# Second half of the first modulation by quarters, a third weight between them, and weight parts one step ahead of the convolutions

## The chip, the cores and the metric

The kernel runs on one core of a Trainium2 chip. Its measure is the device time of one execution in microseconds (us), median of three runs. The core has TensorE (PE, the matrix products), ScalarE (ACT), VectorE (DVE), GpSimd (POOL) and SyncE (SP, which here only issues DMAs); each runs its own list of instructions in order, and they meet at semaphores.

## What is computed

Two transformer blocks follow one another, on one sequence of 256 tokens with 1024 features, in float32. The change lies in the first steps of the first block:

```python
mod = (c_act @ w_ada[l] + b_ada[l])[:, None, :]
shift1, scale1, gate1, shift2, scale2, gate2 = jnp.split(mod, 6, axis=-1)
h = rms_norm(x, norm1_w[l]) * (1.0 + scale1) + shift1
proj = h @ w_in[l]
gq, gk, gv, gz, ga, gb, sq, sk, sv = jnp.split(proj, split_points, axis=-1)
qkv = jax.nn.silu(causal_depthwise_conv(jnp.concatenate([gq, gk, gv], axis=-1), conv_w[l]))
```

`c_act` is one vector of 1024 values, so `scale1` and `shift1` are two vector-matrix products over 8 MB of `w_ada`. Nothing of `h` can be had before they are known for its features, and no product with `w_in` can begin before some of `h` is there. What follows (a gated delta rule, window attention, an MLP, then a second block pair) isn't changed.

## The kernel before

**Weights.** They come as blocks of 1024 KB (`load` on SP, into the three buffers of `raw`). A float32 product is made of three products of rounded parts (`three`, L1715: high by high, high by low, low by high). So each weight block w is split first: ACT writes the high part (`hi(w)`, L669, one instruction of 128x2048), then DVE the low part (`lo(w)`, L1072). Each of the three buffers for parts is used again three blocks later, so `hi(w)` waits until PE is done with block w-3 (`FORMER`, semaphore `block_used`). `h` is split likewise (`h_high`, `first_low`), tile by tile: tile k holds 128 of the 1024 features.

**The start.** PE fills its first microseconds with products of zeros (`warm`). The first modulation is made in two halves of the features. For half 0 and half 1 SP loads four pieces of 1024 KB each (`load_ada`: scale rows 0-511 and 512-1023, then shift rows 0-511 and 512-1023), into the buffers `AT`, `qkT`, `X_inv` and `keys_queries`. For the first three, PE (`ada`, L1827) makes products with four column groups of the array side by side, 512 features wide; ACT copies the rows (`mod_rows_copy`), and PE sums over the partitions and turns them to a column (`row_sums`, 16 one-column matmuls). The fourth piece goes straight to columns (`last_columns`, 64 one-column matmuls). DVE makes scale and shift of it (`first_scales`, `first_shifts`), then `h` (`first_scaled`, `first_low`).

With half 0 known, PE does k = 0 to 3 of the first two weight blocks (`column_half`). k = 4 to 7 of both wait for half 1. The loop `for w in range(6)` follows (L1924): `project(w)` completes block w, a block being 48 matmuls of 256 columns. After block 0 come the gate product (`gab_wh`, `gab_wl`, 24 matmuls) and a small product for a table (`rel_bias`), after block 1 two transposes, after block 4 the sums of the decay (`tri` by `g`, waits `gate_done`). In the middle of block 6, `first_sums` (L2011) waits for `decay_dve`.

**The loop beside it on ACT and DVE.** ACT at step w (L750): `hi(w + 2)`, then the copy of block w out of PSUM into `pad` (waits `block_used`), then `feature(w - 1)`: Silu and, for four of them, Square of the convolution before. DVE at step w (L1218): `lo(w + 2)`, then the convolution of block w, eight instructions (L1233 and L1240; waits `pad_ready` for its block and `feature_ready` for the one before, since both share `cacc`). Step 1 and step 2 hold the gate computation besides, step 5 the difference that gives `decay_dve`. ACT loads function tables where it goes from one function to another (L745, L767, L771).

**SP's order.** `x`, half 0 of the modulation, weights 0 and 1, half 1, then, once the third piece of half 1 has landed, weight 2 and the rest.

Of the kernel before, what the change touches and what calls it, by code (L numbers as in the profile page):

```python
# [9 lines left out]
P = 128  # L10
# [19 lines left out]
FIRST_WEIGHTS = 2  # L30
# [289 lines left out]
def build(nc, stream, x_in, consts_in, vectors_in, gab_in, t5_onehot, t5_log, rel_bias, out):  # L320
    t5_scratch = nc.dram_tensor("t5_scratch", (16, 384), F32, kind="Internal")
    with ExitStack() as ctx:
# [81 lines left out]
        mod_rows = [[inv_b[:, 1024 * i + 512 * u:1024 * i + 512 * u + 512] for u in range(2)] for i in range(2)]  # L404
# [142 lines left out]
        def _(sp):  # L547
# [9 lines left out]
            def load_ada(half, i):  # L557
                if half and i < 3:
                    sp.wait_ge(s.ada_used, i + 1)
                elif half:  # L560
                    sp.wait_ge(s.rows_summed, 2)
                k, c = 4 * (i % 2), 512 * half + (D if i < 2 else 0)
# [10 lines left out]
            for i in range(4):  # L573
                load_ada(0, i)
# [79 lines left out]
        def _(act):  # L654
# [58 lines left out]
            def mod_rows_copy(half, u):  # L713

                act.wait_ge(s.ada_used, 3 * half + (3 if u else 2))
                act.activation(mod_rows[half][u], B[u][:, :], ACT.Copy).then_inc(s.rows_copied, 1)

            def first_highs(w, quarters):
                r = weight_load(w)
                act.wait_ge(raw_landed[r % RING], (r // RING + 1) * 16)  # L720
                for q in quarters:
                    act.activation(high_of(w)[:, 2 * q:2 * q + 2, :], raw_of(r)[:, 2 * q:2 * q + 2, :], ACT.Copy).then_inc(s.first_hi, 1)
# [13 lines left out]
            mod_rows_copy(1, 0)  # L736
            mod_rows_copy(1, 1)
            h_high(0, range(4, KD))
# [11 lines left out]
            for w in range(6):  # L750
                hi(w + 2)
# [31 lines left out]
            hi(8)  # L783
# [280 lines left out]
        def _(dve):  # L1064
# [64 lines left out]
            def first_scales(half):  # L1129
                c, at = slice(4 * half, 4 * half + 4), 480 + 8 * half  # L1130
                dve.wait_ge(s.rows_summed, 2 * half + 1)
                link(dve.tensor_tensor(a1[:, c], STAT[:, at:at + 4], b_scale[:, c], ALU.add))
                dve.tensor_tensor(a1[:, c], a1[:, c], vecs("norm1")[:, c], ALU.mult).then_inc(s.mod_ready, 1)

            def first_shifts(half):
                c, at = slice(4 * half, 4 * half + 4), 484 + 8 * half
                dve.wait_ge(s.rows_summed, 2 * half + 2)
                dve.tensor_tensor(mods[:, c], STAT[:, at:at + 4], vecs("b_ada")[:, c], ALU.add).then_inc(s.mod_ready, 1)
                dve.wait_ge(s.mod_ready, 2 * half + 2)

            def h_parts_2():
                dve.wait_ge(s.rstd_ready, 2)
                dve.wait_ge(s.mod_ready, 6)
# [17 lines left out]
            def residual(last):  # L1161

                for m in range(KD):
# [4 lines left out]
                    if m == 0:  # L1168
                        dve.wait_ge(s.mod_ready, 5)
# [39 lines left out]
            first_scales(1)  # L1209
            first_shifts(1)  # L1210
            for k in range(4, KD):
                first_scaled(k)
                if k > 4:
                    first_low(k - 1)
            first_low(KD - 1)


            for w in range(6):  # L1218
# [5 lines left out]
                lo(w + 2)  # L1224
# [62 lines left out]
            lo(8)  # L1287
# [416 lines left out]
        def _(pe):  # L1704
# [16 lines left out]
            def column_half(w, bank, ks):  # L1721

                if ks[0] == 4:
                    pe.wait_ge(s.lo_ready, w + 1)
                wh = high_of(w)
                wl = low_of(w)
                for k in ks:
                    if k in (0, 2):
                        pe.wait_ge(s.first_lo, 3 * w + k // 2 + 1)
                    pe.wait_ge(s.h_lo_ready, k + 1)  # L1730
# [96 lines left out]
            def ada(half, i):  # L1827

                pe.wait_ge(ada_landed[i], 16 * (half + 1))
                if half and i % 2 == 0:  # L1830
# [726 lines left out]
```

## Time and profile before

| | us |
|---|---|
| median of 3 runs | 991.53 (991.39 to 992.0) |
| the profiled execution | 990.9 |
| its span in the profile | 989.1 |
| PE busy | 978.5 (99%) |
| DVE busy | 607.8 (61%) |
| ACT busy | 476.8 (48%) |

The profile has the time of each instruction on each engine. Times in its rows count from the start of the span. A row of the timeline is one run of like instructions: start, length, engine, line, operation, output and inputs, how many; a bracket at its end gives the idle time of the engine just before, and what ended it. A busy PE need not be a useful one: `zero_r` products count as busy. Line numbers are those of the kernel before.

### The profile page before, as it was taken

What the parts mean: (1) busy time and instruction counts of PE and PEld (TensorE: products, weight loads), DVE (VectorE), ACT (ScalarE), POOL (GpSimd) and SP (SyncE); (2) the same over time, 40 slices, a digit from 0 to 9 for tenths busy, and PEclk for the clock granted to TensorE, in tenths of its full rate; (3) what the DMA queues carried; (4) which work ended last, traced back from release to release, by engine and by line L of the source; (5) the groups of instructions that cost most, each with busy time, mean ns of one, the idle gap of its engine ahead of it and who ended that gap; (6) DMA issues with size and microseconds to landing.
All of it is one profiled execution on the core that took longest, in us unless ns stands there. A gap on an engine that the chain in (4) does not pass through costs nothing.

```text
span 989.1 us, 15628 instructions
## 1 busy us (share of the span) xinstructions
PE 978.5 (99%) x6703; PEld 847.0 (86%) x6703; DVE 607.8 (61%) x750; ACT 476.8 (48%) x640; POOL 36.8 (4%) x37
## 2 busy tenths in 40 slices
PE   9999999999999999999999999999999999999998
PEld 6799988978888888999888888889999888888886
DVE  2589988775665454787754545365876663545444
ACT  3485277454343435533354344446655563435343
POOL 0000560010000000000000000000000000000000
PEclk9999999999999999999999999999999999999999
DMA  9757324775767354446544645454643435454621
GB/s 345 284 191 259 122 87 151 270 243 214 278 217 285 132 211 172 171 171 214 211 145 153 216 167 206 177 191 153 226 156 130 139 144 185 180 204 166 216 86 43
DMA packets 31588, 185.70 MB, mean 188 GB/s; under 512 B 3040, under 2 KB 5536, under 8 KB 10784
## 3 DMA queue, kind: packets, MB, share of 16 engines
q1 hardware_dynamic: 29984, 180.37, 51.0%
q0 software_dynamic: 832, 3.17, 1.0%
q8 instruction: 53, 0.87, 0.3%
q10 hardware_dynamic: 704, 1.17, 0.3%
q14 instruction: 15, 0.12, 0.0%
HBM read 183.62 MB, written 1.07 MB: 187 GB/s over the span
## 4 chain that ended last, share of the span: by engine, by line
PE 98%; DVE 1%; ACT 0%; issue 0%; POOL 0%; DVEq 0%; POOLq 0%
PE bank L1706 51%; PE acc L1706 43%; PE bank L2308 1%; PE bank L2086 1%; PE bank L1802 0%; PE acc L1802 0%; PE acc L2086 0%; PE bank L2166 0%; PE bank L1979 0%; DVE inv_b L1391 0%; DVE norm_tmp L1511 0%; DVE silu_and_hid L1510 0%; DVE inv_b L1384 0%; PE acc L2316 0%; DVE X_inv L1435 0%
## 5 line engine op out<-in xcount | busy, mean ns | idle before, releaser
L1075 DVE TENSOR_TENSOR w_lo<-raw,w_hi 128x2048 fp32r<-128x2048 f32 x144 | 326.9, 2289 | 146.2 <-ACT w_hi L675 146.1
L1706 PE MATMUL bank<-w_hi,h_parts 128*128 128x512 f32 x1056 | 333.5, 391 | 1.3 <-DVE h_parts L1152 1.3
L675 ACT ACTIVATE w_hi<-raw 128x2048 fp32r<-128x2048 f32 x144 | 271.5, 1909 | 102.3 <-PE acc L1706 70.9
L1706 PEld LDWEIGHTS bank<-w_hi,h_parts 128*128 128x128 f32 x1056 | 198.2, 188 | 44.6 <-issue 2.0
L1706 PE MATMUL bank<-w_lo,h_parts 128*128 128x512 f32 x528 | 205.5, 389 | 0.0
L1706 PE MATMUL acc<-h_parts,w_hi 128*128 128x256 f32 x928 | 170.8, 286 | 0.6 <-DVE h_parts L1127 0.6
L1706 PEld LDWEIGHTS acc<-h_parts,w_hi 128*128 128x128 f32 x928 | 143.5, 190 | 5.3 <-issue 3.3
L1706 PE MATMUL acc<-h_parts,w_lo 128*128 128x256 f32 x464 | 131.2, 283 | 0.0
L1706 PE MATMUL acc<-w_hi,o_hi 128*128 128x512 f32 x296 | 119.1, 402 | 0.0
L1706 PEld LDWEIGHTS bank<-w_lo,h_parts 128*128 128x128 f32 x528 | 99.2, 188 | 19.8
L1706 PE MATMUL acc<-w_hi,o_lo 128*128 128x512 f32 x296 | 115.6, 391 | 0.0
L1706 PE MATMUL acc<-w_lo,o_hi 128*128 128x512 f32 x296 | 115.6, 390 | 0.0
L1706 PEld LDWEIGHTS acc<-h_parts,w_lo 128*128 128x128 f32 x464 | 88.0, 190 | 0.0
L927 ACT ACTIVATE silu_and_hid<-bank,rms 128x256 f32<-128x256 f32 x44 | 20.9, 475 | 105.2 <-PE bank L1706 105.2
L1550 DVE TENSOR_TENSOR o_lo<-bank,o_hi 128x512 fp32r<-128x512 f32 x33 | 22.8, 691 | 76.0 <-ACT o_hi L932 76.0
L1706 PEld LDWEIGHTS acc<-w_hi,o_lo 128*128 128x128 f32 x296 | 55.6, 188 | 12.4
L1706 PEld LDWEIGHTS acc<-w_hi,o_hi 128*128 128x128 f32 x296 | 55.6, 188 | 10.9 <-issue 0.2
L1706 PEld LDWEIGHTS acc<-w_lo,o_hi 128*128 128x128 f32 x296 | 55.7, 188 | 10.5
L932 ACT ACTIVATE o_hi<-bank 128x512 fp32r<-128x512 f32 x33 | 19.8, 599 | 75.2 <-PE bank L2308 75.2
L1542 DVE SCALAR_TENSOR_TENSOR silu_and_hid<-bank,rms,silu_and_hid 128x256 f32<-128x256 f32 x44 | 21.2, 481 | 36.6 <-ACT silu_and_hid L927 36.6
L1706 PE MATMUL bank<-h_parts,w_hi 128*128 128x256 f32 x192 | 34.7, 283 | 0.3 <-DVE h_parts L1520 0.3
L1706 PEld LDWEIGHTS bank<-h_parts,w_hi 128*128 128x128 f32 x192 | 29.4, 188 | 0.7 <-DVE h_parts L1520 0.5
(370 smaller groups left out, 993.3 us busy)
## 6 DMA issues: line engine op xcount, KB each, us to landing
raw<-stream SPq DMA_DIRECT2D x162, 1024.0 KB, 5.1
AT<-stream SPq DMA_DIRECT2D x2, 1024.0 KB, 11.8
qkT<-stream SPq DMA_DIRECT2D x2, 1024.0 KB, 13.0
X_inv<-stream SPq DMA_DIRECT2D x2, 1024.0 KB, 14.2
keys_queries<-stream SPq DMA_DIRECT2D x4, 512.0 KB, 12.4
t_tables<-t_scratch POOLq DMA_DIRECT2D x1, 2048.0 KB, 10.2
x_res<-x_in SPq DMA_DIRECT2D x2, 512.0 KB, 5.2
t_tables<-t_scratch POOLq DMA_DIRECT2D x1, 1024.0 KB, 12.4
```

Of the source, the lines that this page charges most:

```text
L675: act.activation(high_of(w), raw_of(r), ACT.Copy).then_inc(s.hi_ready, 1)
L927: act.activation(sg[:, T * t:T * t + T], B[t][:, 0:256], ACT.Silu, scale=rms[:, t:t + 1] if f else 1.0).then_inc(s.silu_ready, 1)
L932: act.activation(hid_parts(j)[0].rearrange("p a b -> p (a b)"), B[2][:, :], ACT.Copy).then_inc(s.hid_hi_ready, 1)
L1075: dve.tensor_tensor(low_of(w), raw_of(weight_load(w)), high_of(w), ALU.subtract).then_inc(s.lo_ready, 1)
L1542: dve.scalar_tensor_tensor(out=o, in0=up, scalar=rms[:, t:t + 1], in1=gate, op0=ALU.mult, op1=ALU.mult).then_inc(s.hid_ready, 1)
L1550: dve.tensor_tensor(low.rearrange("p a b -> p (a b)"), B[2][:, :], high.rearrange("p a b -> p (a b)"), ALU.subtract).then_inc(s.hid_lo_rea ...
L1706: return pe.matmul(o, l, r, start=start, stop=stop, skip_group_check=True)
L2086: ins = pe.transpose(bank[hh][:, P * i:P * i + P], sc[:, hh, P * i:P * i + P], perm)
L2308: ins = pe.transpose(B[2][:, T * i + P * t:T * i + P * t + P], hid[:, T * t + P * i:T * t + P * i + P], ident)
```

## The change

The first half of the modulation and all ahead of it stay. The second half (features 512 to 1023) is cut into two quarters, tiles 4-5 and 6-7. SP loads four pieces of 1024 KB again, now quarter 2 scale, quarter 2 shift, **weight 2**, quarter 3 scale, quarter 3 shift; each piece holds all 1024 rows of 256 features, so a run in memory is 1 KB instead of 2 KB. The fourth piece is done as the others, by `ada_quarter`; `last_columns` is left for half 0 alone. The wait of SP ahead of weight 2 is gone.

PE does k = 0 to 3 of block 2 too, k = 4, 5 of three blocks once quarter 2 is known, and the gate product in three portions (`gab_part`, now in bank `B[3]`); `warm(3)` and `warm(4)` are gone. `project(0)` to `project(2)` then have only k = 6, 7 left. ACT and DVE split blocks 2 and 3 in quarters (`FIRST_WEIGHTS = 4`), block 2 between the steps of the modulation. Block 3's high parts stand at ACT's step 0 of the loop; `hi(w + 3)` and `lo(w + 3)` take the place of `hi(w + 2)` and `lo(w + 2)`, and `hi(8)`, `lo(8)` behind the loop are gone.

```diff
-FIRST_WEIGHTS = 2
+FIRST_WEIGHTS = 4
+EARLY_LOADS = 3
+FEATURES = ((0, 4), (4, 6), (6, 8))
...
-            for i in range(4):
-                load_ada(1, i)
-            sp.wait_ge(ada_landed[2], 32)
-            for i in range(2, len(LOADS)):
+            load_quarter(2, 0)
+            load_quarter(2, 1)
+            load(2)
+            load_quarter(3, 0)
+            load_quarter(3, 1)
+            for i in range(EARLY_LOADS, len(LOADS)):
                 load(i)
...
             for w in range(6):
-                hi(w + 2)
+                if w + 3 < FIRST_WEIGHTS:
+                    first_highs(w + 3, (0, 1, 2, 3))
+                else:
+                    hi(w + 3)
...
-                    act.activation(gabT, B[0][0:16, 0:T], ACT.Copy).then_inc(s.gab_copied, 1)
+                    act.activation(gabT, B[3][0:16, 0:T], ACT.Copy).then_inc(s.gab_copied, 1)
...
-            hi(8)
...
-                lo(w + 2)
+                if w + 3 < FIRST_WEIGHTS:
+                    first_lows(w + 3, (0, 1, 2, 3))
+                else:
+                    lo(w + 3)
...
-            lo(8)
...
+            def ada_quarter(q, u):
+
+                i = 2 * (q - 2) + u
+                pe.wait_ge(ada_landed[i], 32)
+                pe.wait_ge(s.rows_copied, i + 1)
+                for k in range(KD):
+                    at = 32 * (k % 4)
+                    ins = mm(B[u][at:at + 32, 0:256], c_columns[:, k, :], ada_raw[i][:, 256 * k:256 * k + 256], k < 4, k >= 4)
+                ins.then_inc(s.ada_used, 1)
...
-            column_half(0, A[0], range(4))
-            ada(1, 0)
-            column_half(1, A[1], range(2))
-            ada(1, 1)
-            column_half(1, A[1], range(2, 4))
+            column_part(0, range(0, 4))
+            ada_quarter(2, 0)
+            column_part(1, range(0, 2))
             row_sums(1, 0)
-            ada(1, 2)
-            warm(3)
+            column_part(1, range(2, 4))
+            ada_quarter(2, 1)
+            gab_part(range(0, 4))
             row_sums(1, 1)
-            last_columns(1)
-            warm(4)
+            column_part(2, range(0, 4))
+            ada_quarter(3, 0)
+            column_part(0, range(4, 6))
+            row_sums(2, 0)
+            ada_quarter(3, 1)
+            column_part(1, range(4, 6))
+            row_sums(2, 1)
+            column_part(2, range(4, 6))
+            gab_part(range(4, 6))
```

PE before, from the third piece of half 1 to the first products of block 0 with half 1 (`X_inv` and `keys_queries` are the pieces, `inv_b` the copied rows, `zero_r` the zeros, `h_parts` the parts of `h`; names in brackets are semaphores):

```order
L1706 MATMUL bank<-X_inv,c_columns 32x512 [waits rows_copied,ada_landed2]
L1706 MATMUL bank<-X_inv,c_columns 32x512 x3
L1706 MATMUL acc<-zero_r 128x512 x3
L1706 MATMUL bank<-consts,inv_b 64x1 [waits mod_ready,rows_copied]
L1706 MATMUL bank<-consts,inv_b 64x1 x7
L1706 MATMUL bank<-c_act_sb,keys_queries 64x1 [waits ada_landed3]
L1706 MATMUL bank<-c_act_sb,keys_queries 64x1 x15
L1706 MATMUL bank<-c_act_sb,keys_queries 64x1 [waits ada_rest_landed]
L1706 MATMUL bank<-c_act_sb,keys_queries 64x1 x15
L1706 MATMUL acc<-zero_r 128x512 x4
L1706 MATMUL acc<-h_parts,w_hi 128x256 [waits h_lo_ready,lo_ready]
```

PE after the change, from the last piece (quarter 3, shift) on:

```order
L1736 MATMUL bank<-keys_queries,c_columns 32x256 [waits rows_copied,ada_landed3]
L1736 MATMUL bank<-keys_queries,c_columns 32x256 x7
L1736 MATMUL acc<-h_parts,w_hi 128x256 [waits h_lo_ready,first_lo]
L1736 MATMUL acc<-h_parts,w_hi 128x256
L1736 MATMUL acc<-h_parts,w_lo 128x256
L1736 MATMUL acc<-h_parts,w_hi 128x256 x2
L1736 MATMUL acc<-h_parts,w_lo 128x256
```

The 32 one-column matmuls of `last_columns` and the zeros are gone from this place; the piece is now eight matmuls of 256 columns, and products of a weight block stand right behind them.

ACT before, from the last tiles of `h` (`L702`) to the first Silu (`inv_p` is `pad`, `probsT` the gate product's copy):

```order
L702 ACTIVATE h_parts<-norm_tmp 128x256 [waits t_ready] x4
L675 ACTIVATE w_hi<-raw 128x2048 [waits raw_landed2]
L759 ACTIVATE inv_p<-acc 128x2x256 [waits pool_zeroed,block_used]
L764 ACTIVATE probsT<-bank 16x256 [waits gab_product]
L675 ACTIVATE w_hi<-raw 128x8x256 [waits block_used,raw_landed0]
L753 DMA consts<-consts_in 128x1664
L759 ACTIVATE inv_p<-acc 128x2x256 [waits conv_done,block_used]
L745 ACT_TABLE_LOAD
L745 ACTIVATE keys_queries<-XT 128x512 [waits conv_done]
```

ACT after the change, the same place:

```order
L713 ACTIVATE h_parts<-norm_tmp 128x256 [waits t_ready] x2
L736 ACTIVATE w_hi<-raw 128x2x256 [waits block_used,raw_landed0]
L736 ACTIVATE w_hi<-raw 128x2x256 x3
L781 ACTIVATE inv_p<-acc 128x2x256 [waits pool_zeroed,block_used]
L786 ACTIVATE probsT<-bank 16x256 [waits gab_product]
L686 ACTIVATE w_hi<-raw 128x8x256 [waits block_used,raw_landed1]
L775 DMA consts<-consts_in 128x1664
L781 ACTIVATE inv_p<-acc 128x2x256 [waits conv_done,block_used]
L764 ACT_TABLE_LOAD
L764 ACTIVATE keys_queries<-XT 128x512 [waits conv_done]
```

The high part written ahead of the first copy into `pad` was block 2's, with no wait on PE; now it is block 3's, in four instructions, and the first of them waits for `block_used`, that is, for the end of PE's block 0.

## Rows read from the trace of the kernel before

**Rows 1.** The page: busy us, share of the span and instructions of each engine.

```profile
PE 978.5 (99%) x6703; PEld 847.0 (86%) x6703; DVE 607.8 (61%) x750; ACT 476.8 (48%) x640; POOL 36.8 (4%) x37
```

**Rows 2.** PE's waits from 60 to 220 us: total us, times, longest.

```profile
PE bank L1706 <- DVE h_parts L1152: 1.3, 1, 1.3
PE bank L1706 <- DVE X_inv L1435: 1.2, 1, 1.2
```

**Rows 3.** Timeline of PE: start us, us, engine, line, operation, count.

```profile
31.83 1.06 PE L1706 MATMUL bank<-qkT,c_columns 128*32 128x512 f32 x8
...
34.45 0.63 PE L1706 MATMUL bank<-consts,inv_b 128*64 128x1 f32 x16
35.01 1.07 PE L1706 MATMUL bank<-X_inv,c_columns 128*32 128x512 f32 x8
36.00 0.96 PE L1706 MATMUL acc<-zero_r 128*128 128x512 f32 x3
...
37.38 2.01 PE L1706 MATMUL bank<-c_act_sb,keys_queries 128*64 128x1 f32 x64
39.32 1.20 PE L1706 MATMUL acc<-zero_r 128*128 128x512 f32 x4
41.11 0.47 PE L1706 MATMUL acc<-h_parts,w_hi 128*128 128x256 f32 x2 [0.59 <-DVE h_parts L1127]
...
47.69 0.51 PE L1706 MATMUL acc<-h_parts,w_hi 128*128 128x256 f32 x2
...
50.95 0.51 PE L1706 MATMUL acc<-h_parts,w_hi 128*128 128x256 f32 x2
...
68.14 0.73 PE L1706 MATMUL bank<-g,consts 128*128 128x8 f32 x6
...
77.45 1.10 PE L1706 MATMUL bank<-consts,X_inv 128*64 128x2 f32 x32
```

**Rows 4.** Timeline of SP: the issues of two pieces of half 1.

```profile
12.24 0.38 SPq L565 DMA_DIRECT2D AT<-stream  x1
14.81 0.38 SPq L565 DMA_DIRECT2D qkT<-stream  x1
```

**Rows 5.** The same two in the DMA view: KB each, us from issue to landing.

```profile
AT<-stream SPq DMA_DIRECT2D x1, 1024.0 KB, 15.0
qkT<-stream SPq DMA_DIRECT2D x1, 1024.0 KB, 15.1
```

**Rows 6.** Timeline of ACT: high quarters, copies into `pad`, the table, the Silu.

```profile
28.15 1.14 ACT L722 ACTIVATE w_hi<-raw 128x512 fp32r<-128x512 f32 x2
...
50.84 0.60 ACT L759 ACTIVATE inv_p<-acc 128x512 f32<-128x512 f32 x1 [1.61 <-PE acc L1706]
51.46 1.28 ACT L745 ACT_TABLE_LOAD   x1
52.75 0.63 ACT L745 ACTIVATE keys_queries<-XT 128x512 f32<-128x512 f32 x1
...
57.01 0.60 ACT L759 ACTIVATE inv_p<-acc 128x512 f32<-128x512 f32 x1 [1.15 <-DVE XT L1240]
```

**Rows 7.** Timeline of DVE: low quarters, shift, convolutions 0 to 2, gates, decay.

```profile
26.70 3.70 DVE L1190 TENSOR_TENSOR w_lo<-raw,w_hi 128x512 fp32r<-128x512 f32 x6
...
39.44 0.16 DVE L1138 TENSOR_TENSOR mods<-bank,vec 128x4 f32<-128x4 f32 x1 [3.96 <-PE bank L1706]
...
46.45 0.61 DVE L1233 TENSOR_SCALAR XT<-inv_p,vec 128x256 f32<-128x256 f32 x2
...
53.92 0.62 DVE L1233 TENSOR_SCALAR XT<-inv_p,vec 128x256 f32<-128x256 f32 x2 [2.28 <-ACT keys_queries L745]
...
59.54 0.61 DVE L1233 TENSOR_SCALAR XT<-inv_p,vec 128x256 f32<-128x256 f32 x2
...
63.67 0.17 DVE L1269 SCALAR_TENSOR_TENSOR g<-gate_tmp 128x16 f32<-128x16 f32 x1
...
75.87 0.17 DVE L1223 TENSOR_TENSOR kds<-bank,Gs 128x8 f32<-128x8 f32 x1
```

More of the change, by code:

```diff
@@ L555, in load, with load_quarter, load_half @@
                 sp.dma_start(raw[:, i % RING, :], stream[LOADS[i][2]]).then_inc(raw_landed[i % RING], 16)
-            def load_ada(half, i):
-                if half and i < 3:
+            def load_quarter(q, u):
+                i = 2 * (q - 2) + u
+                if i < 3:
                     sp.wait_ge(s.ada_used, i + 1)
-                elif half:
+                else:
                     sp.wait_ge(s.rows_summed, 2)
-                k, c = 4 * (i % 2), 512 * half + (D if i < 2 else 0)
+                c = 256 * q + (0 if u else D)
+                sp.dma_start(ada_raw[i].rearrange("p (k c) -> p k c", k=KD),
+                             stream[0:KD, :, c:c + 256].rearrange("k p c -> p k c")).then_inc(ada_landed[i], 16)
+            def load_half(i):
+                k, c = 4 * (i % 2), D if i < 2 else 0
                 rows = ada_raw[i].rearrange("p (k c) -> p k c", k=4)
@@ L711, in _, with mod_rows_copy @@
             root(0)
-            def mod_rows_copy(half, u):
-                act.wait_ge(s.ada_used, 3 * half + (3 if u else 2))
-                act.activation(mod_rows[half][u], B[u][:, :], ACT.Copy).then_inc(s.rows_copied, 1)
+            def mod_rows_copy(part, u):
+                a, b = FEATURES[part]
+                act.wait_ge(s.ada_used, 2 * part + u + 2)
+                act.activation(mod_rows[part][u], B[u][:, 0:P * (b - a)], ACT.Copy).then_inc(s.rows_copied, 1)
             def first_highs(w, quarters):
@@ L736, in _ @@
             mod_rows_copy(1, 0)
+            first_highs(2, (0, 1))
             mod_rows_copy(1, 1)
-            h_high(0, range(4, KD))
+            h_high(0, range(4, 6))
+            first_highs(2, (2, 3))
+            mod_rows_copy(2, 0)
+            mod_rows_copy(2, 1)
+            h_high(0, range(6, KD))
             dest = [kT[:, 0:2, :], kT[:, 2:4, :], qT[:, 0:2, :], qT[:, 2:4, :], vT[:, 0:2, :], vT[:, 2:4, :]]
@@ L1209, in _ @@
             first_scales(1)
+            first_lows(2, (0, 1))
             first_shifts(1)
[L1211 to L1215, printed above, removed]
+            first_scaled(4)
+            first_scaled(5)
+            first_low(4)
+            first_low(5)
+            first_lows(2, (2, 3))
+            first_scales(2)
+            first_shifts(2)
+            first_scaled(6)
+            first_scaled(7)
+            first_low(6)
+            first_low(7)
             for w in range(6):
@@ L1825, in _, with ada_half @@
             two = lambda b: b[:, :].rearrange("p (a b) -> p a b", a=2)
-            def ada(half, i):
-                pe.wait_ge(ada_landed[i], 16 * (half + 1))
-                if half and i % 2 == 0:
-                    pe.wait_ge(s.rows_copied, 1 + i // 2)
+            def ada_half(i):
+                pe.wait_ge(ada_landed[i], 16)
                 for k in range(4):
@@ L1857, in last_columns, with gab_part @@
                 ins.then_inc(s.rows_summed, 1)
+            def gab_part(ks):
+                pe.wait_ge(s.x_scaled, KD)
+                pe.wait_ge(s.gab_lo, 1)
+                for k in ks:
+                    pe.wait_ge(s.h_lo_ready, k + 1)
+                    a, b = gab_wh[:, 16 * k:16 * k + 16], gab_wl[:, 16 * k:16 * k + 16]
+                    ins = three(B[3][0:16, 0:T], a, b, h_hi[:, k, :], h_lo[:, k, :], k == 0, k == KD - 1)
+                if ks[-1] == KD - 1:
+                    ins.then_inc(s.gab_product, 1)
             def warm(n, bank=A[3]):
@@ L1918, in project @@
                 wait_bank(w)
-                if w < 2:
-                    column_half(w, A[w], range(4, KD))
+                if w < EARLY_LOADS:
+                    column_part(w, range(6, KD))
+                elif w < FIRST_WEIGHTS:
+                    column_part(w, range(KD))
                 else:
@@ L1926, in _ @@
                 if w == 0:
-                    pe.wait_ge(s.gab_lo, 1)
-                    for k in range(KD):
-                        a, b = gab_wh[:, 16 * k:16 * k + 16], gab_wl[:, 16 * k:16 * k + 16]
-                        ins = three(B[0][0:16, 0:T], a, b, h_hi[:, k, :], h_lo[:, k, :], k == 0, k == KD - 1)
-                    ins.then_inc(s.gab_product, 1)
+                    gab_part(range(6, KD))
                     pe.wait_ge(s.t5_loaded, 48)
```

74 lines of the change are left out of this document (40 added, 34 removed).

## The prediction

> **What bounds the kernel now.** The page gives PE 99% of the span [rows 1], but zeros count there, so I read on. PE's waits from 60 to 220 us come to two, 1.3 and 1.2 us [rows 2]; everything else that ACT and DVE do there is ready in time. The kernel is bound by how early PE gets through useful products, and by anything that ACT or DVE deliver late. So I ask two things of the change: how much of PE's time at the start it turns into useful products, and whether ACT and DVE keep up afterwards.
>
> In the timeline of PE [rows 3] the second half of the modulation is seen to cost, between 35.01 and 41.11 us: a piece (0.99), zeros (0.96), the row sums, 64 one-column matmuls for the last piece (2.01 busy, 1.94 to the next row), zeros (1.20) and an idle 0.59 until DVE has `h`. Zeros and the wait are what a filled schedule can win.
>
> **Prices on PE.** Blocks 2 to 4 are 144 matmuls of 256 columns from 50.95 to 68.14, 0.1194 us each [rows 3]. A piece of 512 columns takes 0.99 (35.01 to 36.00); with 12 matmuls behind it 2.62 (31.83 to 34.45), so 0.19 more go where products follow a piece. I take that gap behind row sums as well, bounds 0 and 0.19. Sixteen row-sum matmuls take 0.56 (34.45 to 35.01); a quarter has eight, 0.30. A piece by quarters is twice as many matmuls of half as many columns. The same columns stream, so 0.99 is the lower bound; if each cost as much as a wide one it would be 1.98. I take 1.0, since 64 one-column matmuls in 1.94 us show that issuing costs only 0.03 each.
>
> **PE in the new order.** Up to the point 31.83 both orders have done the same (12 products of block 1 behind the first piece). From there to the end of block 0 the new order has 102 products (12.18: 12 of block 1, 12 of the gates, 24 of block 2, 12 each of blocks 0, 1 and 2 with quarter 2, 6 gates, 12 of block 0 with quarter 3), three pieces (3.0), four row sums (1.2) and six gaps (1.14): 17.5, so block 0 ends at about **49.35**, against 44.0 before (41.11 plus 24 products). I call this moment t0. Behind it come 6 gate products (0.72), the table product (0.80: 6.58 from 41.11 to 47.69 less 48 products), 12 products with the transposes (1.82, half of the products of 47.69 to 50.95 and all of its rest), and 12 more: 4.85. Block 2 ends at 54.2, before at 56.7 (50.95 plus 48 products). **PE is 2.5 us ahead.**
>
> **What covers it.** The last shift and `h` behind it take 1.67 us (39.44 [rows 7] to 41.11 [rows 3]); the new order has 12 products of block 2, a gap and 6 of the gates there, 2.34, so no wait, 0.67 to spare. Quarter 2's shift has 24 products of block 2 and a piece over it. DMA: pieces of 2 KB runs land at 27.24 and 29.91 (12.24 + 15.0, 14.81 + 15.1) [rows 4, 5], 2.67 apart. For 1 KB runs the bounds are 2.67 (bytes decide) and 5.34 (runs decide); bytes are the nearer by far if 12 MB are to flow as they do, and I take 3.0. Weight 2 ahead of quarter 3 then puts the last piece near 39, and PE wants it at 42.6. Only above some 3.9 us for a piece would PE wait. SP loses a wait and gains one load that has none; behind it weight 3 lands near 42, long before t0. Cost zero.
>
> **ACT and DVE behind t0.** Here I find the price. Block 0 ends 5.3 us later than before, and the first convolution needs it. And ACT stands with block 3's high parts ahead of the copy into `pad`, and these wait for the same end of block 0. So the copy and all behind it on ACT (the gate copy, `hi(4)`, the first Silu) are pushed back. Step by step from t0:
>
> - Four high quarters at 0.55 (two in 1.14 with a tail [rows 6]), DVE's four low quarters at 0.62 (six in 3.70 [rows 7]) run one behind; the last low ends at 0.05 + 3 x 0.62 + 0.60 + 0.62 = 3.15. The copy is done at 2.85. Convolution 0 starts at t0 + 3.15.
> - A convolution's start to the next copy: 3.09 (53.92 [rows 7] to 57.01 [rows 6]). Copy to the end of the first Silu, with the table load between: 50.84 to 53.38 [rows 6], 2.54. Convolution 1 starts at t0 + 8.8. Before, 53.92 came 0.54 after that Silu's end with nothing named for the difference; bounds 0 and 0.54, I take 0 for a plain hand-over.
> - Convolution 1 to 2: 5.62 (53.92 to 59.54 [rows 7]), DVE's own work (convolution, gates, a whole low part). Same in the new order: t0 + 14.4.
> - Convolution 2 to `gate_done`: 59.54 to 63.84 (63.67 + 0.17), 4.3: **t0 + 18.7**.
> - Convolution 2 to `decay_dve`: 59.54 to 76.04 (75.87 + 0.17), 16.5: **t0 + 30.9**. ACT and DVE go through the same list here, one block number on.
>
> PE wants `gate_done` behind block 4, at t0 + 4.85 + 96 x 0.1194 = t0 + 16.3. It waits 2.4. Before it came with the decay sums at 68.14 [rows 3], when `gate_done` was 4.3 old. From there to `first_sums` PE takes 9.31 (68.14 to 77.45): t0 + 28.0. `decay_dve` comes at t0 + 30.9: it waits 2.9 again. Before, the spare was 77.45 - 76.04 = 1.4. So `first_sums` starts at 49.35 + 30.9 = 80.25, before at 77.45: **2.8 us later**, though PE was 2.5 ahead at 54. Queued behind the two waits is everything on PE.
>
> **Afterwards.** DVE is 4.2 us late at convolution 2 (63.75 for 59.54) and stays so through the loop; `lo(8)` is no longer behind it, which takes out some 2.2 (5.62 less 3.09 for a convolution and some 0.3 of gates), so DVE is then no later than PE. A lost time on PE is only won back where PE waited before, and there are 2.5 us of that in 160 [rows 2], both for work of DVE that itself hangs on PE. I count nothing back. Sum against the profiled execution: 990.9 + 2.8 = 993.7; against the median (0.6 above it) 991.53 + 2.8 = **994.3**.
>
> **A rule beside the trace.** In the trace a table load lasts 1.28 us and the Silu starts 1.29 us after it (51.46, 52.75) [rows 6]. The Trainium skill, in "ScalarE: Activation LUTs", section "What ACT_TABLE_LOAD costs", adds a drain of about 1380 ns to every switch, 2.66 us in all. By that rule the first Silu, which the new order puts on the path to PE, would end 1.4 later and the sum would be 995.7; by the row it stays at 994.3. No drain is seen in this row, so I go by the row.
>
> **The rivals.**
>
> - *Faster: the chain behind t0 is shorter than PE's road.* If PE reached the decay sums and `first_sums` with both semaphores set, its 2.5 us would stay, 989.0. For it: both waits had spare before (4.3 and 1.4), and ACT and DVE are one part ahead. Against it: the spare of 1.4 must cover a chain that begins 5.3 later and PE that is 2.5 earlier. It turns at `decay_dve` 28.1 after t0 (77.45 less 49.35): below that no loss; the whole gain needs `gate_done` below 16.3 and `decay_dve` below 25.6. I count 18.7 and 30.9.
> - *No change that can be measured.* t0 earlier by up to 1.1 (no gaps), the four low quarters overlapping better, or a start of convolution 1 that doesn't hang on the whole row of copy, table and Silu: each takes 0.5 to 1.1 off the 2.8. Time 991.6 to 993.4, middle 992.6.
> - *Slower still: quarter pieces at 1.98 instead of 1.0.* The narrow matmuls don't overlap as the wide ones do. Four of them move t0 by 3.9, and both chains with it: 998.2; at half of that 996.2. A lower granted clock in the stretch would act alike.
> - *The pieces land late.* At 5.34 each, the last lands near 48 and PE waits some 5 us ahead of it; t0 moves as far, 999. The 1 KB run would have to cost as much as the 2 KB run.
>
> **How the numbers follow.** A measurement of this kernel tells from no change about 0.2%, 2 us, so 989.5 to 993.5 is "same". The forecast (2.8, bounds 1.9 to 4.0 from the 0.54 and the gaps) has 0.56; no measurable change 0.24; faster 0.12; slower pieces or late ones 0.08. Slower by over 0.2% is 0.56 + 0.08, and a part of the forecast that falls just under 2 us goes to "same": 0.62. Same 0.26, faster 0.12. The range leaves out the faster case and the far ends of the last two: 990.8 to 996.3.
>
> **What would show it.** Right: PE at work without a gap from 24 to about 66 us; block 0's copy into `pad` near 51.6 and convolution 0 near 52.5; an idle PE of about 2.4 us at 66 ahead of the `tri` products, released by DVE's `g`, and one of about 2.9 at 77 ahead of the `X_inv` sums, released by DVE's `kds`; `first_sums` at 80.25; everything from there on later by the same. Wrong: no idle PE at these two places; a piece that takes 1.5 or more; a wait for `AT`, `qkT`, `X_inv` or `keys_queries`; convolution 1 well ahead of 58. If the two waits are there and the end isn't later, time was won back behind 80 us, and my reading of the spare is what failed.

## The result and the profile after

The changed kernel takes **994.86 us** (median of 22 runs, 992.73 to 998.79), the kernel before 992.13 in the same comparison (22 runs, 989.35 to 995.07): a ratio of 1.003, 95% interval 1.002 to 1.004. Forecast were 994.3 and a range of 990.8 to 996.3, with 0.62 for slower. The profiled execution took 994.79, its span is 993.0, so 3.9 longer than the profiled one before. Two more comparisons later gave 1.0033 (1.0019 to 1.0048) and 1.0024 (1.001 to 1.0038).

The page, to set beside [rows 1]: PE issues 31 instructions fewer and is as busy as before.

```profile
PE 978.1 (98%) x6672; PEld 846.6 (85%) x6672; DVE 608.7 (61%) x759; ACT 477.0 (48%) x648; POOL 36.8 (4%) x37
```

PE's waits from 20 to 220 us (total, times, longest). The second and third are those of [rows 2]; the first and the fourth are new, and they are the two that were forecast (2.4 and 2.9).

```profile
PE bank L1736 <- DVE g L1300: 2.8, 1, 2.8
PE bank L1736 <- DVE h_parts L1173: 1.3, 1, 1.3
PE bank L1736 <- DVE X_inv L1465: 1.2, 1, 1.2
PE bank L1736 <- DVE kds L1251: 1.1, 1, 1.1
PE acc L1736 <- DVE w_lo L1211: 0.6, 1, 0.6
```

PE's timeline after, which answers [rows 3] (the rows show two records for each of the program's float32 matmuls, so x16 is the piece's eight and x8 a quarter's four one-column ones): three of the four pieces by quarters and the one-column sums, the first gate product behind block 0 (49.62), the table product (50.42), the two waits, and a product far behind them.

```profile
29.59 1.14 PE L1736 MATMUL bank<-AT,c_columns 128*32 128x256 f32 x16
...
34.23 1.07 PE L1736 MATMUL bank<-qkT,c_columns 128*32 128x256 f32 x16
35.23 0.41 PE L1736 MATMUL bank<-h_parts,gab_wh 128*16 128x256 f32 x2
...
42.72 0.40 PE L1736 MATMUL bank<-consts,inv_b 128*64 128x1 f32 x8
43.05 1.07 PE L1736 MATMUL bank<-keys_queries,c_columns 128*32 128x256 f32 x16
...
49.62 0.39 PE L1736 MATMUL bank<-h_parts,gab_wh 128*16 128x256 f32 x2
...
50.42 0.81 PE L1736 MATMUL bank<-XT,rel_bias_sb 32*16 32x384 f32 x2
...
69.08 0.81 PE L1736 MATMUL bank<-g,consts 128*128 128x8 f32 x6 [2.75 <-DVE g L1300]
...
71.62 0.63 PE L1736 MATMUL acc<-h_parts,w_hi 128*128 128x256 f32 x2
...
81.17 1.10 PE L1736 MATMUL bank<-consts,X_inv 128*64 128x2 f32 x32 [1.14 <-DVE kds L1251]
...
153.13 1.09 PE L1736 MATMUL bank<-consts,X_inv 128*64 128x128 f32 x16 [1.22 <-DVE X_inv L1465]
```

A piece takes 1.00 (34.23 to 35.23), the row sums of a quarter 0.33. `first_sums` stands at 81.17, before at 77.45 [rows 3]. Before, the last of these products stood here, as far behind `first_sums` as it does after (71.96):

```profile
149.41 1.09 PE L1706 MATMUL bank<-consts,X_inv 128*64 128x128 f32 x16 [1.22 <-DVE X_inv L1435]
```

ACT and DVE after, from the end of block 0, beside [rows 6] and [rows 7]: ACT with block 3's high quarters, the copy into `pad`, and the table load with the first Silu; then DVE with block 3's low quarters, convolutions 0 to 2, `g` and `kds`.

```profile
49.88 2.19 ACT L736 ACTIVATE w_hi<-raw 128x512 fp32r<-128x512 f32 x4 [2.39 <-PE acc L1736]
51.98 0.58 ACT L781 ACTIVATE inv_p<-acc 128x512 f32<-128x512 f32 x1
...
56.36 0.60 ACT L781 ACTIVATE inv_p<-acc 128x512 f32<-128x512 f32 x1 [1.49 <-DVE XT L1271]
56.98 1.28 ACT L764 ACT_TABLE_LOAD   x1
58.27 0.63 ACT L764 ACTIVATE keys_queries<-XT 128x512 f32<-128x512 f32 x1
```

```profile
50.55 2.50 DVE L1211 TENSOR_TENSOR w_lo<-raw,w_hi 128x512 fp32r<-128x512 f32 x4 [2.59 <-ACT w_hi L736]
52.96 0.61 DVE L1264 TENSOR_SCALAR XT<-inv_p,vec 128x256 f32<-128x256 f32 x2
...
59.01 0.62 DVE L1264 TENSOR_SCALAR XT<-inv_p,vec 128x256 f32<-128x256 f32 x2 [0.86 <-ACT keys_queries L764]
...
64.62 0.61 DVE L1264 TENSOR_SCALAR XT<-inv_p,vec 128x256 f32<-128x256 f32 x2
...
68.75 0.17 DVE L1300 SCALAR_TENSOR_TENSOR g<-gate_tmp 128x16 f32<-128x16 f32 x1
...
80.95 0.17 DVE L1251 TENSOR_TENSOR kds<-bank,Gs 128x8 f32<-128x8 f32 x1
```

One thing was not forecast. Behind the first wait the matmuls of blocks 5 and 6 are slow for 3 to 4 us (the row at 71.62: 0.63 for 0.40). The windows show the granted clock (third number from the right) at 0.50 there, the lower of its two levels, 1.2 GHz:

```profile
69.00:71.00 2.00, 1.92 (x16) 1.96 (x17) 0.77 (x1) 1.98 (x3) 0.05 (x1) 0.94 0.06 16
71.00:73.00 2.00, 2.00 (x11) 2.00 (x11) 1.79 (x2) 1.96 (x3) 0.00 (x0) 0.50 0.00 0
73.00:75.00 2.00, 2.00 (x14) 2.00 (x14) 2.00 (x7) 2.00 (x2) 0.00 (x0) 0.71 0.72 180
```

**Questions.** Theory A: what sets the time is the chain on ACT and DVE that begins at the end of block 0, which the new order moves back. Theory B: the loss stands ahead of the end of block 0, in quarters and sums. Theory C: it is the clock behind the new wait.

### The profile page after: what moved, and what is told of

The parts are those of the page before. It is cut to its first block, busy times and chain, and to the rows that moved or that the text cites. A ratio compares the mean times of both kernels' runs of the same rounds, so it can differ in the third digit from the quotient of the medians.

```text
span 993.0 us, 15616 instructions
## 1 busy us (share of the span) xinstructions
PE 978.1 (98%) x6672; PEld 846.6 (85%) x6672; DVE 608.7 (61%) x759; ACT 477.0 (48%) x648; POOL 36.8 (4%) x37
## 4 chain that ended last, share of the span: by engine, by line
PE 93%; DVE 3%; DMA 1%; ACT 1%; issue 1%; SPq 0%; DVEq 0%; ACTq 0%
PE bank L1736 50%; PE acc L1736 39%; PE bank L2363 1%; DMA X_inv<-stream 1%; DVE XT L1271 1%; PE bank L2141 1%; PE bank L1833 0%; DVE w_lo L1211 0%; PE acc L1833 0%; DVE XT L1264 0%; PE acc L2141 0%; ACT L764 0%; PE bank L2221 0%; DVE w_lo L1096 0%; ACT w_hi L686 0%
## 5 line engine op out<-in xcount | busy, mean ns | idle before, releaser
L1096 DVE TENSOR_TENSOR w_lo<-raw,w_hi 128x2048 fp32r<-128x2048 f32 x142 | 322.3, 2288 | 146.7 <-ACT w_hi L686 146.6
L686 ACT ACTIVATE w_hi<-raw 128x2048 fp32r<-128x2048 f32 x142 | 267.6, 1909 | 104.6 <-PE acc L1736 70.5
L1736 PE MATMUL acc<-h_parts,w_hi 128*128 128x256 f32 x928 | 173.8, 289 | 0.7 <-DVE w_lo L1211 0.6
L1736 PEld LDWEIGHTS acc<-h_parts,w_hi 128*128 128x128 f32 x928 | 145.5, 192 | 4.9 <-issue 2.7
## 6 DMA issues: line engine op xcount, KB each, us to landing
keys_queries<-stream SPq DMA_DIRECT2D x1, 1024.0 KB, 13.9
```

The source lines that it names most:

```text
L686: act.activation(high_of(w), raw_of(r), ACT.Copy).then_inc(s.hi_ready, 1)
L1096: dve.tensor_tensor(low_of(w), raw_of(weight_load(w)), high_of(w), ALU.subtract).then_inc(s.lo_ready, 1)
L1736: return pe.matmul(o, l, r, start=start, stop=stop, skip_group_check=True)
```

## Experiments

For every kernel I read four moments of PE: the first piece of quarter 2 (29.59 after, 29.22 before), the table product T (50.42, 46.94), `first_sums` F (81.17, 77.45) and the last product shown above, X (153.13, 149.41). The first moment shifts between executions of the same kernel (28.05 to 29.59 for the changed one); the distances agree to 0.1 us, except where a cause is named below. The column us has the run's median and behind it that of the kernel before measured together with it.

| kernel | piece to T | T to F | F to X | us | ratio to before (95%) |
|---|---|---|---|---|---|
| before | 17.72 | 30.51 | 71.96 | 992.13 | |
| after | 20.83 | 30.75 | 71.96 | 994.86 | 1.003 (1.002-1.004) |
| after_again | 20.76 | 30.83 | 71.96 | 995.67 / 991.78 | 1.0033 (1.0019-1.0048) |
| after_third_time | 20.76 | 30.74 | 73.48 | 995.00 / 992.08 | 1.0024 (1.0010-1.0038) |
| undo_ahead | 20.76 | 29.64 | 71.96 | 993.65 / 991.78 | 1.0014 (1.0002-1.0027) |
| third_early | 20.76 | 29.12 | 71.96 | 994.19 / 991.78 | 1.003 (1.0018-1.0043) |
| third_early_conv_first | 20.75 | 25.92 | 72.50 | 990.06 / 991.78 | 0.9983 (0.9969-0.9997) |
| conv_first_again | 20.76 | 25.91 | 72.28 | 989.99 / 992.08 | 0.9979 (0.9966-0.9993) |
| high_twice_after | 20.74 | 32.81 | 71.98 | 996.96 / 992.85 | 1.0063 (1.0043-1.0083) |
| high_twice_before | 17.62 | 30.50 | 71.95 | 992.64 / 992.85 | 1.0006 (0.9991-1.0021) |
| after_preload | 20.75 | 29.82 | 71.96 | 993.67 / 992.85 | 1.0019 (1.0006-1.0032) |
| warm_in_wait | 20.76 | 30.76 | 73.48 | 997.72 / 992.85 | 1.0061 (1.0043-1.0078) |
| warm_in_both | 20.76 | 30.75 | 71.95 | 994.14 / 992.08 | 1.0020 (1.0007-1.0032) |
| block2_behind | 18.09 | 30.75 | 73.49 | 993.80 / 992.08 | 1.0014 (1.0001-1.0027) |

### 1. The changed kernel again, and the step ahead undone

> The changed kernel beside the others on one chip. It is the measure for them: 2.7 us above the kernel before, as its 22 runs gave. In the trace PE should again wait for the gates (2.8 us near 66) and for the decay difference (1.1 us near 80).

It was 3.9 over the kernel before, for 2.7. PE waited 2.76 for `g`, but not for `kds`, and yet F stood 30.83 behind T, for 30.75. By the windows the granted clock was 0.50 for about 6.8 us behind the wait for `g` here, and for about 3.4 in the first profile; PE was then so late that it came to `first_sums` (79.64) just behind `kds` (79.34, 0.17 long). So the chain on DVE sets the moment as before, and the clock can use up the whole of the second wait.

> The changed kernel with one part undone: later parts are again made two blocks ahead of the convolution in hand (block 3's high part at step 1 of the loop, whole; parts 8 behind the loop), so ACT's first act after block 0 is the copy into pad. All of the PE order, the quarters and the early third weight stay. Theory A (the chain copy, table, Silu, convolution behind the end of block 0 sets the time): convolution 1 starts some 2.4 us nearer to the end of block 0 (6.2 for 8.6 to 9.4), so the wait for the decay difference ends some 2.2 us earlier; against that PE waits about 1 us for block 3's low part. Net 1.5 to 2.4 us faster than the changed kernel, about 0.5 us above the kernel before. Rival B (what is lost is lost ahead of the end of block 0, in pieces, switches or late data): no faster than the changed kernel. Rival C (the clock, which falls after the 2.8 us idle, is the price): faster by what of that idle goes, with a granted clock of 1.00 from 70 to 75.

```diff
-FIRST_WEIGHTS = 4
+FIRST_WEIGHTS = 3
...
-                if w + 3 < FIRST_WEIGHTS:
-                    first_highs(w + 3, (0, 1, 2, 3))
-                else:
-                    hi(w + 3)
+                if w:
+                    hi(w + 2)
```

(`lo` likewise; `hi(8)` and `lo(8)` stand behind the loop again.) It was 2.0 us below the changed kernel measured beside it, as expected. Convolution 0 waits for the copy into `pad`, no longer for low parts, and convolution 1 begins 6.6 after the end of block 0 (9.4 in the changed kernel). PE now waits for low parts, 2.7 us in all (1 expected), and no more for `g` or `kds`: one bound has taken the place of the other, 1.1 us of T to F lower. The clock fell here too, to 0.50 for about 3.4 us from 69 us on, behind the last of these waits (1.31); `kds` was ready 1.8 before `first_sums`, so no later wait took that up, and it is part of the 29.64. Of theory C that much holds in this kernel. The waits of this kernel and DVE at convolutions 0 and 1:

```profile
PE acc L1734 <- DVE w_lo L1095: 2.7, 3, 1.3
```

```profile
48.75 0.62 DVE L1261 TENSOR_SCALAR XT<-inv_p,vec 128x256 f32<-128x256 f32 x2 [2.49 <-ACT inv_p L779]
...
54.48 0.62 DVE L1261 TENSOR_SCALAR XT<-inv_p,vec 128x256 f32<-128x256 f32 x2 [0.54 <-ACT keys_queries L764]
```

### 2. Block 3's parts made inside the modulation

> The changed kernel, but block 3's parts are made before block 0 is done, in idle time of ACT and DVE (near 41 to 49 us), into room of two buffers that are free by then; so nothing of it stands between the end of block 0 and the copy into pad. The loop's order stays otherwise. Theory A: copy into pad right at the end of block 0, convolution 0 some 2.6 us nearer, but ACT still does block 4's high part ahead of the second copy and waits for block 1 first, so convolution 1 only 1.2 us nearer; in all 1.2 us (0.8 to 1.6) faster than the changed kernel. B: no faster. C: faster only by what the clock gives back, nothing if the wait for the decay difference still covers it.

```diff
+            with ExitStack() as early:
+                third_parts = [sb(n, [P, BLOCK], F32R, early) for n in ("third_hi", "third_lo")]
...
             mod_rows_copy(2, 0)
+            first_highs(3, (0, 1))
             mod_rows_copy(2, 1)
+            first_highs(3, (2, 3))
...
-                if w + 3 < FIRST_WEIGHTS:
-                    first_highs(w + 3, (0, 1, 2, 3))
-                else:
+                if w:
                     hi(w + 3)
```

Block 3's parts lie in the memory of `AT` and `qkT`, which are free by then, so they needn't wait for block 0. ACT has its weight at 41.99, and piece to T stays at 20.76: they cost nothing ahead of block 0. T to F falls by 1.6 to 29.12, PE's wait for `g` to 1.4. The median is 1.5 below the changed kernel measured beside it, as expected; the two ratios, 1.003 and 1.0033, don't separate them. I take the trace's 1.6 for what it does to this stretch, and leave open how much of it the time keeps.

### 3. The convolutions ahead of the next parts

> As third_early, and in every step of the loop the copy, the Silu and the convolution stand ahead of the weight parts; the decay difference stands right behind convolution 4; the Silu table is loaded once before block 0 ends. Theory A: convolution 1 starts 4.9 us after the end of block 0 (9.4 in the changed kernel), the gates are ready before PE wants them, PE waits under 0.5 us in both places and keeps the 2.5 us of its denser start: 4 to 5 us faster than the changed kernel, 1.5 to 2.2 us faster than the kernel before. B: it stays at or above the kernel before. C: the same as A in sign, since there is no idle and no fall of the clock; but then undo_ahead should gain only what the clock costs.

> The kernel with the third block's parts made inside the modulation and each convolution ahead of the next block's parts, once more, beside the others of this call: 1 to 2.5 us below the kernel before, 4 to 6 below the changed kernel.

```diff
+            link(act.activation(root_tmp[:, :], ones, ACT.Silu))
             for w in range(6):
-                hi(w + 3)
...
                 if w:
                     feature(w - 1)
+                    hi(w + 3)
```

On top of experiment 2: ACT loads the Silu's table ahead of block 0's end, and DVE's low parts stand behind the convolution of their step. DVE's order in four rows: convolution 0 waits for the copy alone, convolution 1 follows in 4.3 (6.1 in the changed kernel), and `g` and `kds` come before PE wants them.

```profile
48.58 0.62 DVE L1263 TENSOR_SCALAR XT<-inv_p,vec 128x256 f32<-128x256 f32 x2 [1.33 <-ACT inv_p L786]
52.92 0.62 DVE L1263 TENSOR_SCALAR XT<-inv_p,vec 128x256 f32<-128x256 f32 x2 [1.34 <-ACT keys_queries L773]
...
63.17 0.17 DVE L1306 SCALAR_TENSOR_TENSOR g<-gate_tmp 128x16 f32<-128x16 f32 x1
...
73.67 0.17 DVE L1282 TENSOR_TENSOR kds<-bank,Gs 128x8 f32<-128x8 f32 x1
```

PE's waits to 145 us are small ones, none for `g` or `kds`:

```profile
PE acc L1743 <- DVE w_lo L1102: 0.9, 1, 0.9
PE acc L1743 <- DVE w_lo L1217: 0.8, 1, 0.8
PE acc L1743 <- DVE h_parts L1154: 0.3, 1, 0.3
```

T to F is 25.92, the clock 1.00 all the way to 95 us. In both comparisons the kernel is **faster than both others**, by 1.7 and 2.1 us than before and by 5.6 and 5.0 than the changed one. Of the 4.8 that T to F is shorter than in the changed kernel, 0.3 to 0.5 go again by X; where wasn't looked into. This is the rival "faster" of the prediction made true: the useful products in the gaps do bring time, once the chain behind block 0 is short. A kernel before with only its chain shortened wasn't run; PE waits for nothing of that chain there (from its first piece to F its one wait is 0.59, for `h` [rows 3]), so little could come of it.

### 4. Two microseconds more on ACT, behind block 0 and in the same place before

> The changed kernel with block 3's high parts made twice on ACT: one more copy of 128x2048 (1.90 us, with its wait for itself about 2.0) right behind the end of block 0, ahead of the four copies, of the low parts and of pad(0). Theory A: the whole chain starts 2.0 us later and nothing of it is spare, since PE waits for both g and kds: conv0, g and kds 2.0 us later, the time 1.8 to 2.2 us over the changed kernel's. Theory B and theory C: the chain has room behind block 0, at most 0.7 us over it.

> The kernel before with the high parts of the block that stands in the same place (block 2) made twice on ACT, 2.0 us more ahead of pad(0) and of the low parts of block 2. Theory A: there the chain has room: conv0 comes 2.0 us later, but conv1 waits for the evacuation of block 1, which waits for PE till 50.84, so that conv1 comes only about 0.6 us later, and PE, which waits for neither g nor kds there, loses 0 to 0.6 us of the time. A time 1.5 us or more over the kernel before would say that the chain was as tight there, and that theory A has the wrong reason.

```diff
+                if w == 3:
+                    link(act.activation(high_of(w), raw_of(r), ACT.Copy))
                 for q in quarters:
```

(before: the same line for block 2.) In the changed kernel T to F grew by 2.06. The chain is 1.6 of it: counted from T, convolution 0 came 1.95 later, convolution 1 and `kds` 1.6, since 0.3 were made up between convolution 0 and the next copy (3.08 for 3.40). The other 0.4 is PE's: the clock stayed low for about 6.8 us behind the wait for `g`, as in `after_again`, and PE reached `first_sums` half a microsecond after `kds`, with no wait. PE and DVE there:

```profile
70.52 1.42 PE L1738 MATMUL bank<-g,consts 128*128 128x8 f32 x6 [2.59 <-DVE g L1302]
...
83.04 1.10 PE L1738 MATMUL bank<-consts,X_inv 128*64 128x2 f32 x32
```

```profile
82.38 0.17 DVE L1253 TENSOR_TENSOR kds<-bank,Gs 128x8 f32<-128x8 f32 x1
```

The median stood 4.1 over the kernel before, where the changed kernel's stood 2.7 to 3.9 in its three comparisons: 0.2 to 1.4 more, less than the 1.8 to 2.2 expected, from six runs with a wide interval. In the kernel before, convolution 1 and `kds` came 0.7 later (53.92 to 54.64, 75.87 [rows 7] to 76.58), and T, F and X stood where they had stood, to 0.01 us. DVE and PE there:

```profile
54.64 0.62 DVE L1235 TENSOR_SCALAR XT<-inv_p,vec 128x256 f32<-128x256 f32 x2 [0.95 <-ACT keys_queries L747]
...
76.58 0.17 DVE L1225 TENSOR_TENSOR kds<-bank,Gs 128x8 f32<-128x8 f32 x1
```

```profile
149.40 1.09 PE L1708 MATMUL bank<-consts,X_inv 128*64 128x128 f32 x16 [1.22 <-DVE X_inv L1437]
```

The same work in the same place moves `first_sums` by 2.06 us after and by nothing before. That the chain became the bound is shown by this pair. Of 2.0 us before, 1.3 went in ACT's wait for block 1 (1.61 [rows 6]) and 0.7 in the spare of 1.4 that the prediction had counted.

### 5. The table load taken off the chain

> The changed kernel with one activation of one column (Silu) right behind the high parts of h, in ACT's idle time ahead of the end of block 0, so that the table of Silu is loaded there and not between pad(1) and the first Silu (1.28 us at 56.98). Theory A: conv1 waits for that Silu 0.86 us longer than for the low parts of block 4, so it comes 0.86 us sooner, and the time is 0.4 to 0.9 us below the changed kernel's. Theory B: the same time as the changed kernel.

```diff
             h_high(0, range(6, KD))
+            link(act.activation(root_tmp[:, :], ones, ACT.Silu))
```

Convolution 1 came 7.67 after T, for 8.59: 0.92 sooner, and T to F fell by 0.93, so it is the chain that carries it. The load itself is 1.28 again and the Silu began 1.29 after it (56.98, 58.27 above). With the load gone convolution 1 is held by the low part ahead of it, which is why 0.9 and not 1.3 came off; 0.3 of the 0.9 stands between convolution 0 and the copy (3.07 for 3.40), ahead of where the load was. In time the kernel is 0.8 over the kernel before, where the changed kernel stood 2.7 to 3.9 over: 1.9 to 3.1 less, for 0.4 to 0.9 expected. The trace explains 0.9 of that. The rule of the Trainium skill, "ScalarE: Activation LUTs", section "What ACT_TABLE_LOAD costs", by which a drain of about 1380 ns comes on top, would put the Silu 2.66 after the load began; this trace doesn't agree either.

### 6. The clock

> The changed kernel with eleven more products of zeros on PE (128x512 each, about 0.21 us at the full clock, 2.4 us in all) between project(4) and the wait for g. They fill the gap of 2.75 us that stands there in the changed kernel, behind which the granted clock fell to 0.50 for some 3 us and PE lost about 1.5 us in blocks 5 and 6. Theory A (the chain on DVE and ACT behind the end of block 0 sets the time): the clock stays at 1.00, PE reaches the wait for kds about 1.5 us sooner, that wait grows from 1.1 to about 2.6 us, and the time stays that of the changed kernel within 0.4 us. Theory B (the loss stands ahead of the end of block 0): the same time too. Theory C (the fall of the clock behind the new wait is what costs): 1.2 to 1.6 us faster than the changed kernel.

```diff
                     pe.wait_ge(s.masks_loaded, 16)
+                    warm(11, B[3][:, :])
                     pe.wait_ge(s.gate_done, 1)
```

This one I had wrong. With PE kept busy the clock held behind `g`, and the wait for `kds` grew to 2.72 as expected; but then the clock fell behind that wait. PE at both places and the windows behind the second:

```profile
67.47 0.83 PE L1736 MATMUL bank<-g,consts 128*128 128x8 f32 x6
...
79.66 1.10 PE L1736 MATMUL bank<-consts,X_inv 128*64 128x2 f32 x32 [2.72 <-DVE kds L1251]
```

```profile
80.00:82.00 2.00, 2.00 (x32) 1.98 (x31) 2.00 (x3) 0.53 (x2) 0.00 (x0) 0.71 0.26 102
82.00:84.00 2.00, 2.00 (x12) 2.00 (x11) 2.00 (x7) 0.00 (x0) 0.00 (x0) 0.50 0.58 127
```

F to X is 73.48 for 71.96: 1.52 lost, with no wait behind it to take it up. The time was 997.72, 4.9 over the kernel before, where the changed kernel's is 2.7 to 3.9 over. Theory C as it stood falls (no gain from holding the clock), and so does my "same time". What took its place: a fall costs nothing if a later wait takes it up, and 1.5 us if none does.

> The changed kernel with eleven products of zeros in front of the wait for g and eleven more in front of the wait for kds. With the first eleven alone the clock held behind the wait for g, but then fell for 4 us behind the wait for kds, which had grown to 2.72 us, and the time was 2 to 3 us over the changed kernel's where the same had been expected. If that fall is what it cost (theory C in a narrower form: a fall costs nothing where a later wait takes it up, and all of it behind the last wait): the clock is 1.00 from 60 to 90 us, the first sums come 30.8 us after the relative-bias product as before, and the time is 1.2 to 2 us below that with the first eleven alone, within 0.5 us of the changed kernel's. If the products of zeros themselves cost the time: as slow as with eleven, or slower.

```diff
                     pe.wait_ge(s.masks_loaded, 16)
+                    warm(11, B[3][:, :])
                     pe.wait_ge(s.gate_done, 1)
...
             def first_sums():
+                warm(11, B[3][:, :])
                 pe.wait_ge(s.decay_dve, 1)
```

The clock is 1.00 from 20 to 95 us, F to X is back at 71.95, T to F still 30.75. The time, 994.14, is 0.9 below the changed kernel measured beside it (within 0.5 was expected). Over the kernel before it stands 2.1, the run with one filled wait 4.9; the traces explain 1.5 of these 2.8. The rest isn't placed, but the profile of `warm_in_wait` is of the fastest of its six runs (994.76, mean granted clock 0.996), and the two slowest, 999.5 and 999.7, have 0.991: the clock was low for longer in them than the profile shows.

### 7. Block 2's products put back behind block 1

> The changed kernel with the products of block 2 (36 pairs' worth of k = 0 to 5, 4.3 us of PE) taken out of the modulation and made behind block 1, as before the change; the quarters, the parts in quarters and the step ahead stay. Theory A (what the change moved ahead of block 0 delays the chain behind it): block 0 ends 2 to 3 us sooner (not the whole 4.3, since PE then waits for h), PE no longer waits for g and waits 1 us or so for kds, and the time is 1.5 to 3 us below the changed kernel's. Theory B (the quarters, with their pieces and sums, are what moves block 0's end): block 0's end moves by under 0.7 us and so does the time.

> The changed kernel once more, so that the others of this call have it beside them: 2 to 4 us over the kernel before. Theory A: the first sums 30.8 us after the relative-bias product, whatever the clock did before and between.

```diff
-            column_part(2, range(0, 4))
...
-            column_part(2, range(4, 6))
...
-                if w < EARLY_LOADS:
+                if w < 2:
                     column_part(w, range(6, KD))
```

Block 0 ends 2.7 us sooner (piece to T 18.09 for 20.76), and PE waits twice for `h`, where block 2's products had been the cover. The wait for `g` is gone, that for `kds` 1.5:

```profile
PE acc L1736 <- DVE h_parts L1148: 1.6, 2, 0.9
PE bank L1736 <- DVE kds L1251: 1.5, 1, 1.5
```

T to F is 30.75 again, though PE does different work in it: the chain's own length. Theory B has the remaining 0.4 of the 3.0 by which piece to T grew; theory A has 2.7. But the chain begins at the end of block 0, and that moved by 5.2 from the first piece (14.8 to 20.0), not by 3.0: 2.1 more are the 18 gate products that stood behind block 0 before and stand ahead of it now. No run put these back alone. In time this kernel was 1.2 us below the changed kernel measured beside it and not 1.5 to 3; the clock fell behind its wait for `kds` (F to X 73.49), but it did so in the profile of that changed kernel too.

## Why the prediction was right, and where it was not

- **Prices on PE.** A piece by quarters costs 1.00 (taken 1.0), sums 0.33 (0.30). From the first piece to the end of block 0 are 20.03 us (49.62 less 29.59), predicted 20.13. This is the step that everything hangs on, and the rival of slow pieces is out. Block 0 ended at 49.62 for 49.35 because this execution had begun its first piece 0.37 later.
- **Cover.** No wait for `h` or for a piece after 24 us, bar 0.6 for block 0's low parts. The cover was worth what was said: without it 1.6 (experiment 7).
- **DMA.** Weight 2 (issued at 21.10) and quarter 3's pieces (24.66, 25.14) took 11.9, 11.3 and 13.9 us from issue to landing, by the rows below; they landed at 33.0, 36.0 and 39.0, 3.0 apart, as taken, and the last near 39, as said. Weight 3 landed at 41.5.

```profile
raw<-stream SPq DMA_DIRECT2D x1, 1024.0 KB, 11.9
X_inv<-stream SPq DMA_DIRECT2D x1, 1024.0 KB, 11.3
keys_queries<-stream SPq DMA_DIRECT2D x1, 1024.0 KB, 13.9
```

- **The chain behind t0.** Convolution 0 at t0 + 3.34 (3.15), convolution 1 at + 9.4 (8.8), then 5.61 (5.62) to convolution 2, 4.30 (4.3) to `gate_done` and 16.5 (16.5) to `decay_dve`. The 0.6 at convolution 1 is the term that was undersized: 0.2 ahead of the low quarters (ACT began 0.26 after t0, for 0.05; the four low quarters took 2.50 as priced), 0.3 between convolution 0 and the next copy into `pad` (3.40 for 3.09; 3.07 to 3.09 in `undo_ahead`, `high_twice_after` and `after_preload`, and nothing in the traces names the cause), and a hand-over of 0.1 out of the 0.54 that I had bounded and taken at 0. `gate_done` came at t0 + 19.3 and `decay_dve` at + 31.5.
- **The waits.** `g`: 2.75 for 2.4, at 66.3, as said. `kds`: 1.14 for 2.9, since the fall of the clock had made PE late by about 1.5; with the clock held it was 2.72. The size was wrong in a place where it didn't count, because DVE sets the moment and PE only how long it waits.
- **The end.** `first_sums` was predicted 2.8 later and came 3.7 later: 0.4 from the start of this execution, 0.6 from the chain, less 0.1. By distances from the first piece it is 3.3 (3.1 up to T, 0.2 from T to F). Told by the chain: block 0 ends 5.2 later, the chain from there to `kds` is 0.5 shorter (31.3 for 31.8), and 1.4 is the spare. The medians say 2.7, 3.9 and 2.9. That 2.7 meets the forecast's 2.8 so closely in the first of them is in part luck, since the chain was priced 0.6 too short.
- **Nothing won back.** F to X is 71.96 in both profiles, and from X to the end 839.9 and 839.7.
- **The no-change rival** needed a start of convolution 1 that doesn't hang on copy, table and Silu. Experiments 2 and 5 took parts of that row away and got 1.6 and 0.9 of T to F.

## What to carry to other kernels

Before you fill an engine's gaps with work that comes ahead of a milestone, look at who starts from that milestone: 6.4 us of useful products (4.3 of block 2, 2.1 of the gates), put ahead of the end of block 0, made the engine early by 2.5 at the end of block 2 and the start of the chain late by 5.2, and the chain had 1.4 to spare. Count its links against the moment at which the busy engine wants each result, and take off the chain what needn't be in it (parts of later blocks, a table load) before moving anything. A delay of known size, put into the same place of both kernels, tells in two runs which of them has slack there.

## What the hardware showed that I had not expected

- **The clock falls behind waits of one to three us in the middle of dense work.** Behind the wait for `g` (1.4 to 2.8 us) it went to 0.50 in the changed kernel's three profiles and in those of experiments 2, 4 and 5, by the windows for about 3.4 us in four of them and for about 6.8 in two (`after_again`, `high_twice_after`); the length of the wait doesn't tell which (2.75 and 2.76 in `after` and `after_again`). It also fell behind the wait of 1.31 in `undo_ahead`. Behind waits of 1.1 to 1.5 for `kds` it fell in some executions (after_third_time, block2_behind) and not in others (after, third_early). A fall of 3.4 us costs 1.5 us where nothing takes it up: F to X has only two values in all kernels that do the same work there, 71.96 and 73.48, to 0.03. From X to the end there are two as well, 839.7 to 839.9 and 841.4 to 841.7 (after_again, after_third_time, undo_ahead, conv_first_again), with the clock low at 145 to 160 us in the latter: behind the wait of 1.2 that every kernel has there. That may be a part of the 5 us by which runs of one kernel differ. Their times do go with the clock: of 35 runs of the kernel before, measured beside experiment 1, those with a mean granted clock of 0.999 took up to 990.3 us and the two at 0.991 took 995.0 and 995.2. Which waits decide it wasn't tested.
- **One issue on SP can take longer than two loads are apart.** An issue that took 0.38 before [rows 4] took 6.63 in the changed kernel. That the 1 KB runs do it isn't shown: in the kernel before, the next piece, with 2 KB runs, took 3.10 to issue (at 18.03). PE waited for none of these loads (ACT for weight 2, 1.8 us), and they landed evenly, 3.0 apart; whether a shorter issue would have brought them sooner wasn't tried.

```profile
11.86 0.38 SPq L567 DMA_DIRECT2D AT<-stream  x1
14.43 6.63 SPq L567 DMA_DIRECT2D qkT<-stream  x1
```
